# Half-array low-rank products, layer norms inside the last feed-forward, and an early read-back before the RWKV scan

## The reference

```python
a  = sigmoid(a0 + (xa @ a1) @ a2)                    # a1: 1024x64, a2: 64x1024
wl = w0 + tanh(xw @ w1) @ w2                         # twice: forward and backward, rank 64 each
g  = sigmoid(xg @ g1) @ g2                           # rank 128
kk = k * k_k, normalised per head of 64 channels
y  = scan over the tokens, forward and backward, with decay exp(-exp(.)) of each wl
```

```python
x   = layernorm(ALPHA * x + mixed @ w_out, ln1_g, ln1_b)
ffn = (silu(x @ w_gate) * (x @ w_up)) @ w_down       # hidden width 2816
x   = layernorm(ALPHA * x + ffn, ln2_g, ln2_b)       # the result
```

## Time and profile before

| | |
|---|---|
| median of three runs | 4254.95 us (4245.76 to 4255.61) |
| the profiled execution's own time | 4248.42 us |
| its span, first to last instruction | 4246.4 us, mean granted TensorE clock 0.961 |
| PE busy | 3944.9 us, 93% (weight loads 72%) |
| DVE, ACT, POOL busy | 54%, 31%, 31% |
| DMA | 361.79 MB, mean 85 GB/s |
| low-rank stage, first to last of its matmuls | 1688.0 to 1765.0 us |
| PE idle between projections and scan | 1855.8 to 1878.7 us |
| last product of the merge to first of ffn4 | 3814.5 to 3845.0 us |
| end of the last product to the end of the span | 4208.1 to 4246.4 us |

### The profile page before, as it was taken

One profiled execution on the slowest core, in us unless ns is written; L12 is line 12 of the kernel. 1 busy time (PEld: TensorE's weight loads), 2 busy tenths in 40 slices (PEclk: granted clock), 3 DMA queues, 4 the chain that ended last, 5 costly groups with the idle time before them and its releaser, 6 DMA issues. The chain is left out here.

```text
span 4246.4 us, 63005 instructions
## 1 busy us (share of the span) xinstructions
PE 3944.9 (93%) x26276; PEld 3050.7 (72%) x26276; DVE 2297.8 (54%) x3285; ACT 1310.6 (31%) x2106; POOL 1326.2 (31%) x521
## 2 busy tenths in 40 slices
PE   8999999998999998978888999899999999998997
PEld 6855788756658886456775788667777877876885
DVE  5646577466647755448885667465541526252033
ACT  3345333232213333334444333222222111103222
POOL 1011444413114440000001344345554343654442
PEclk9999999999999999889998999989999999998999
DMA  5310222222112222341112122212122121222221
GB/s 168 122 58 21 99 99 99 104 99 85 55 62 96 99 99 100 121 181 46 43 43 85 60 99 96 83 65 80 60 80 73 66 75 67 102 99 80 93 87 58
DMA packets 43517, 361.79 MB, mean 85 GB/s; under 512 B 4419, under 2 KB 4803, under 8 KB 23820
## 3 DMA queue, kind: packets, MB, share of 16 engines
q1 hardware_dynamic: 43276, 358.32, 23.3%
HBM read 334.71 MB, written 23.59 MB: 84 GB/s over the span
## 5 line engine op out<-in xcount | busy, mean ns | idle before, releaser
L266 POOL TENSOR_TENSOR ffn_weights_low<-weight_ring,ffn_weights_high 128x2048 fp32r<-128x2048 f32 x128 | 601.2, 4697 | 767.3 <-ACT ffn_weights_high L343 766.6
L192 PE MATMUL banks<-ffn_in_high,ffn_weights_low 128*128 128x512 f32 x2048 | 802.9, 392 | 31.0 <-DVE ffn_in_low L425 13.4
L193 PE MATMUL banks<-ffn_in_low,ffn_weights_high 128*128 128x512 f32 x2048 | 800.2, 391 | 0.0
L194 PE MATMUL banks<-ffn_in_high,ffn_weights_high 128*128 128x512 f32 x2048 | 799.8, 391 | 0.0
L192 PEld LDWEIGHTS banks<-ffn_in_high,ffn_weights_low 128*128 128x128 f32 x2048 | 386.4, 189 | 117.4 <-POOL ffn_weights_low L277 26.0
L193 PEld LDWEIGHTS banks<-ffn_in_low,ffn_weights_high 128*128 128x128 f32 x2048 | 386.6, 189 | 80.8 <-issue 0.7
L194 PEld LDWEIGHTS banks<-ffn_in_high,ffn_weights_high 128*128 128x128 f32 x2048 | 386.5, 189 | 80.8
L343 ACT ACTIVATE ffn_weights_high<-weight_ring 128x2048 fp32r<-128x2048 f32 x128 | 245.1, 1915 | 560.1 <-PE banks L194 560.1
L3386 POOL TENSOR_TENSOR third_weights_low<-weight_ring,third_weights_high 128x1024 fp32r<-128x1024 f32 x144 | 365.3, 2537 | 11.5
L460 DVE SCALAR_TENSOR_TENSOR ffn_gate<-ffn_up,columns_sb,ffn_gate 128x511 f32<-128x511 f32 (+1 forms) x132 | 277.6, 2103 | 161.4 <-ACT ffn_value L373 161.4
L3384 POOL CAST third_weights_high<-weight_ring 128x1024 fp32r<-128x1024 f32 x144 | 158.7, 1102 | 547.9 <-PE banks L194 499.7
(11 more groups left out here) (594 smaller groups left out, 7377.5 us busy)
## 6 DMA issues: line engine op xcount, KB each, us to landing
weight_ring<-weights SPq DMA_DIRECT2D x144, 2048.0 KB, 7.7
scan_in<-rwkv_operands SPq DMA_DIRECT2D x8, 1280.0 KB, 8.4
rwkv_operands<-rwin_staged SPq DMA_DIRECT2D x24, 256.0 KB, 3.2
scan_in<-rwkv_operands SPq DMA_DIRECT2D x8, 512.0 KB, 3.9
bias_tiles<-bias_rows SPq DMA_DIRECT2D x8, 448.0 KB, 8.8
residual<-x SPq DMA_DIRECT2D x4, 512.0 KB, 7.3
filt_decay<-decay SPq DMA_DIRECT2D x1, 2048.0 KB, 8.2
rwkv_residual<-residual SPq DMA_DIRECT2D x1, 2048.0 KB, 7.1
```

What stands on the lines that cost most here:

```text
L192: pe.matmul(out, w[1], x[0], start=start, stop=False, skip_group_check=True)
L193: pe.matmul(out, w[0], x[1], start=False, stop=False, skip_group_check=True)
L194: return pe.matmul(out, w[0], x[0], start=False, stop=stop, skip_group_check=True)
L266: pool.tensor_tensor(parts[1], landed, parts[0].bitcast(F32), ALU.subtract).then_inc(S["split"], 1)
```

## The change

**Low-rank pairs on row halves.** The two w1 matrices lie side by side in the weight chunk, a1 is laid twice, so that 24 matmuls of 128 columns replace 32; both halves of `al` and `decay` are filled. w2 of both directions stand on the two partition halves, and a2's column tiles alternate between the halves. The 24 output matmuls are issued two by two, `half(n)` being rows 0 to 63 or 64 to 127. The gather of the head sums is done twice, to partitions 0 to 15 and 64 to 79, so that the inverse norms stand on both halves; the spreads come two by two after two output matmuls. The spread matrix is loaded to both halves. ACT copies and casts whole 128-partition tiles. Bank numbers shift by one (`A2 = 3`).

**Read-back at the seam.** The scan's operand tile (`T.operands`, seven tiles) is shared with the projection, which uses it for the low-rank ring, `tanh` and `rstd`. Values are evacuated into `G.hT`. Behind its last weight load SP loads the reset row into `G.x`, then tile 0's decays and first three operands; it spills the gains of tiles 1 to 7, copies gain 0 and value 0 from SBUF to SBUF, and issues the value spills of tiles 1 to 7 with a semaphore (`T.v_spilled`) on which the block does not wait: SP waits for it in the scan before tile 1's load, DVE before it writes the first output. The scan's block starts with the mask load, without loads for tile 0.

**Layer norms inside ffn4.** `layer_norm` and `store` go; `feed_forward(..., norms=("ln1", "ln2"))` takes their work. Centring is one operation with the total in PSUM as operand. Squares are summed by 64-column matmuls that alternate between output partitions 0 to 63 and 64 to 127. DVE copies that bank, four matmuls with one column turn the sums into a 128x4 tile, on which variance, root and reciprocal work, and four matmuls with a broadcast operand and the identity spread it back; scaling reads it from PSUM. On ACT the casts of the first eight weight pieces and of the next half stand ahead of the root, two pieces ahead of the squares. Shift and cast of an input tile follow each other tile by tile.

**Down projection, in all four feed-forwards.** The last two hidden tiles are done together, bank by bank. In ffn4 DVE adds a running total behind each residual add, and one ones-matmul sums it. The output is stored in four DMAs, each after two shifted tiles.

```diff
+def norm_pe(pe, G, N, sq, gathered, inverse, bank):
+    for k in range(KT):
+        side = slice(k % 2 * (P // 2), (k % 2 + 1) * (P // 2))
+        pe.wait_ge(N["squared"], k + 1)
+        mm = pe.matmul(G.banks[side, bank, :], G.con("ones")[:, 0:P // 2], sq[:, k, :], start=(k < 2), stop=(k >= KT - 2))
+        if k >= KT - 2:
+            mm.then_inc(N["square_sums"], 1)
+    pe.wait_ge(N["gathered"], 1)
+    for j in range(JT):
+        mm = pe.matmul(G.banks[:, bank + 1, j:j + 1], gathered[:, j * P:(j + 1) * P], G.con("ones")[:, 0:1], start=True, stop=True)
+    mm.then_inc(N["columns"], 1)
+    pe.wait_ge(N["rstd_done"], 1)
+    for j in range(JT):
+        of = inverse[:, j:j + 1]
+        of = bass.AP(tensor=of.tensor, offset=of.offset, ap=[of.ap[0], [0, P]])
+        mm = pe.matmul(G.banks[:, bank + 2, j * P:(j + 1) * P], of, G.con("ident"), start=True, stop=True)
+    mm.then_inc(N["spread"], 1)
...
+def norm_centre(dve, G, N, total_bank):
+    for k in range(KT):
+        dve.scalar_tensor_tensor(out=G.x[:, k, :], in0=G.banks[:, total_bank, :], scalar=-1.0 / D, in1=G.x[:, k, :],
+                                 op0=ALU.mult, op1=ALU.add).then_inc(N["centred"], 1)
+def norm_dve(dve, G, N, gathered, inverse, bank):
+    dve.wait_ge(N["square_sums"], 2)
+    dve.tensor_copy(gathered[:, :], G.banks[:, bank, :]).then_inc(N["gathered"], 1)
+    dve.wait_ge(N["columns"], 1)
+    dve.tensor_scalar(inverse[:, :], G.banks[:, bank + 1, 0:JT], 2.0 / (P * D), LN_EPS, ALU.mult, ALU.add).then_inc(N["var_done"], 1)
+    dve.wait_ge(N["root_done"], 1)
+    dve.reciprocal(inverse[:, :], inverse[:, :]).then_inc(N["rstd_done"], 1)
+    dve.wait_ge(N["spread"], 1)
...
@@ feed_forward, SP
+            if norms:
+                for k in range(0, KT, 2):
+                    sp.wait_ge(N_out["shifted"], k + 2)
+                    sp.dma_start(G.aps["out"][k * P:(k + 2) * P, :].rearrange("(k p) n -> p k n", p=P), G.x[:, k:k + 2, :]).then_inc(S["stored"], 16)
@@ feed_forward, PE, down projection
-            for t in range(FT):
+            for t in range(FT - 2):
...
+            pe.wait_ge(S["split"], up_halves + down_halves)
+            pe.wait_ge(S["tile_split"], FT)
+            for m in (*range(4, KT), *range(4)):
+                for t in (FT - 2, FT - 1):
+                    at = t % 2 * D + m * P
+                    mm = exact_product(pe, G.banks[:, m, :], [w[:, t // 2 % 2, at:at + P] for w in w_parts],
+                                       tile_parts(t), start=False, stop=(t == FT - 1))
+                mm.then_inc(S["down_done"], 1)
@@ feed_forward, ACT
+            if norms:
+                pieces(range(2))
+                norm_squares(act, G, N_in, sq)
+                pieces(range(2, KT))
+                high(0, 0, 1, True)
+                norm_root(act, N_in, inverse)
@@ rwkv_projection, PE
-            for l, outs in enumerate(((A1,), (W0, W1), (G1,))):
+            for l in (A1, W1, G1):
...
+                for n in range(2):
+                    mm = pe.matmul(G.banks[heads(n), SUM_BANK, :], gather(m), xx_squares(m), start=(m == 0), stop=(m == KT - 1))
...
+            for n in range(A2, N_OUT, 2):
+                lora_out(n)
+                lora_out(n + 1)
                 if n >= DECAY + KT:
+                    unit_spread(n - DECAY - KT)
+                    unit_spread(n - DECAY - KT + 1)
@@ rwkv_projection, SP
+            sp.dma_start(T.operands[:, 5:7, :], of[:, 5:7, :]).then_inc(S["operands_in"], 16)
+            sp.dma_start(T.operands[:, 0:3, :], of[:, 0:3, :]).then_inc(S["operands_in"], 16)
...
+            sp.dma_start(T.operands[:, 3, :], b[:, 0, :]).then_inc(S["operands_in"], 16)
...
+            sp.dma_start(T.operands[:, 4, :], G.hT[:, 0, :]).then_inc(S["operands_in"], 16)
```

More of the change, by code:

```diff
@@ L207, in row_unit @@
     return G.chunk(c, KT)[:, 2 * u:2 * u + 2, :]
-def feed_forward(G, name, gain, taps, act_func, shift=0, keep=1.0):
+NORM = ("centred", "squared", "square_sums", "gathered", "columns", "var_done", "root_done", "rstd_done", "spread", "scaled", "shifted")
+def norm_pe(pe, G, N, sq, gathered, inverse, bank):
[15 more added lines that the diff above has]
+    mm.then_inc(N["spread"], 1)
@@ L214, in feed_forward, with norm_scale @@
+def norm_scale(dve, G, N, gain, bank, k):
+    dve.scalar_tensor_tensor(out=G.x[:, k, :], in0=G.x[:, k, :], scalar=G.col(gain, k), in1=G.banks[:, bank + 2, :],
+                             op0=ALU.mult, op1=ALU.mult).then_inc(N["scaled"], 1)
+def feed_forward(G, name, gain, taps, act_func, shift=0, keep=1.0, norms=()):
     nc = G.nc
@@ L414, in _ @@
                 high(n // 2 % 2, n // 4, n % 2, False)
+            if norms:
+                norm_squares(act, G, N_out, sq)
+                norm_root(act, N_out, inverse)
+                for k in range(KT):
+                    norm_shift(act, G, N_out, norms[1] + "_b", k)
         @block.vector
@@ L488, in _, with total @@
                 tile_low(t)
-            for n, m in enumerate((*range(4, KT), *range(4))):
+            order = (*range(4, KT), *range(4))
+            def total(n):
+                dve.wait_ge(S["added"], n + 1)
+                if n > 1:
+                    dve.wait_ge(S["totalled"], n - 1)
+                dve.tensor_tensor(square_sum, G.x[:, order[0], :] if n == 1 else square_sum, G.x[:, order[n], :], ALU.add).then_inc(S["totalled"], 1)
+            for n, m in enumerate(order):
                 dve.wait_ge(S["down_done"], n + 1)
@@ L492, in _ @@
                                          op0=ALU.mult, op1=ALU.add).then_inc(S["added"], 1)
+                if norms and n > 1:
+                    total(n - 1)
+            if norms:
+                total(KT - 1)
+                dve.wait_ge(S["total_summed"], 1)
+                norm_centre(dve, G, N_out, 4)
+                norm_dve(dve, G, N_out, rstd, inverse, 5)
+                for k in range(KT):
+                    norm_scale(dve, G, N_out, norms[1] + "_g", 5, k)
         G.first += UP_CHUNKS + DOWN_CHUNKS
@@ L2216, in _, with lora_out @@
                 pe.wait_ge(S["keys_squared"], m + 1)
-                mm = pe.matmul(G.banks[0:2 * KT, SUM_BANK, :], gather(m), xx_squares(m), start=(m == 0), stop=(m == KT - 1))
+                for n in range(2):
+                    mm = pe.matmul(G.banks[heads(n), SUM_BANK, :], gather(m), xx_squares(m), start=(m == 0), stop=(m == KT - 1))
             mm.then_inc(S["head_sum"], 1)
-            pe.wait_ge(S["select"], 32)
+            pe.wait_ge(S["select"], 48)
             arrived(pe, W2_CHUNK)
             w2 = G.ring[:, G.slot(W2_CHUNK), :]
-            for n in range(A2, N_OUT):
+            def lora_out(n):
                 if n >= LBANKS:
@@ L2448, in rwkv_scan @@
     with ExitStack() as ctx:
-        S = stage(G, "scan", ctx, "masks_loaded", "reset_loaded", "go", *PER, *PER_TURN)
-        ld = G.sb("scan_in", [P, SPILLED, SEQ], ctx=ctx)
+        S = stage(G, "scan", ctx, "masks_loaded", "go", *PER, *PER_TURN)
+        ld = T.operands
         ex = G.x[:, 0:5, :]
@@ L3285, in rwkv @@
         T.g2 = G.sb("rwkv_g2", [P, D], ctx=ctx)
-        rwkv_projection(G, T)
-        rwkv_scan(G, T)
+        T.v_spilled = ctx.enter_context(nc.semaphore("rwkv_v_spilled"))
+        with ExitStack() as inner:
+            T.operands = G.sb("scan_in", [P, SPILLED, SEQ], ctx=inner)
+            rwkv_projection(G, T)
+            rwkv_scan(G, T)
         rwkv_output(G, T)
@@ L4281, in third_block @@
             gated_merge(G, T)
-    layer_norm(G, "ln1", "ln1_g", "ln1_b", total_summed=True)
-    feed_forward(G, "ffn4", None, None, ACT.Silu, keep=ALPHA)
-    layer_norm(G, "ln2", "ln2_g", "ln2_b")
-def store(G):
-    nc = G.nc
-    with ExitStack() as ctx:
-        S = stage(G, "store", ctx, "stored")
-        block = ctx.enter_context(nc.Block())
-        @block.sync
-        def _(sp):
-            sp.dma_start(G.aps["out"].rearrange("(k p) n -> p k n", p=P), G.x[:, :, :]).then_inc(S["stored"], 16)
-            sp.wait_ge(S["stored"], 16)
+    feed_forward(G, "ffn4", None, None, ACT.Silu, keep=ALPHA, norms=("ln1", "ln2"))
 def three_blocks_kernel(nc, aps, layout):
```

228 lines of the change are left out of this document (107 added, 121 removed).

## The result

The changed kernel takes 4197.3 us (median of 4 runs, 4194.5 to 4201.8), the kernel before 4250.4 on the same chip (4 runs, 4244.9 to 4255.6): ratio 0.9871, 95% interval 0.9858 to 0.9885, 1.3% faster. A second series of the same kernel gave 0.9883 (0.9861 to 0.9905). The forecast was 4200. The profiled execution took 4198.8, span 4196.7, 49.7 us less than before.

What follows compares the result with a forecast made beforehand. PE was 93% busy, so time could come only from stretches where it stands or runs slow: 28.0 + 5.0 + 6.8 + 11.9 = 51.7 us less, forecast 4200 us, 8-in-10 range 4183 to 4222.

Steps and rivals of the forecast that it cites:

- Low-rank stage, -28.0: Low-rank stage: merged input, overlapping output pairs and a free gather bring the second projection 28.0 us earlier.
- the last four rounds [...] are about 2.2 us each on PE at 2.4 GHz: Low-rank output: four closing rounds of two row-half pairs and two tile-size switches, 2.2 us each, hidden but for 0.5.
- rival A: Low-rank output: the clock falls in the last four rounds, 17.6 us instead of 8.8; +7.3, 4207 us; chance 0.19.
- the 1.5 kept back: Low-rank stage: 1.5 us held back from the 29.5 us gain for the clock, leaving 28.0.
- Seam, -5.0: Seam to the scan: PE starts when the masks land, 1873.7 instead of 1878.7, -5.0 us.
- that wait is DMA rate: Seam to the scan: 5,888 KB in the DMA queue set the block's end, only 0.6 us less than before.
- ln1, -6.8: Layer norm into the last feed-forward: first product at 3838.3 instead of 3844.99, -6.8 us.
- So the first split waits: Last feed-forward: POOL's subtraction, running to 3837.6, holds back DVE's first split; first product 3838.3 instead of 3836.8.
- The end, -11.9: Final norm and store: first scale 4223.8 instead of 4232.1, store in four ending at 4234.5, -11.9 us.
- B: Scan seam and last feed-forward: masks land no earlier, first splits wait for two POOL operations; 4209 us; chance 0.09.
- C: Low-rank stage: pairs do not overlap in a stream; 28 us lost and 5 of the squares, 4233 us; chance 0.06.
- D: From the gather on: half-array matmuls run one by one at 1.2 GHz; +20.5, 4275 us; chance 0.04.

Runs made afterwards that it cites:

- wide spreads: Changed kernel with the eight head-norm spreads contracting over 64 rows instead of 16; time not distinguishable from the changed kernel's, the intervals overlap.
- same-half run: Changed kernel with both matmuls of each low-rank output pair contracting over rows 0 to 63; run once, 4216.7 us.

## Why the prediction was right, and where its steps were off

The way and the places of the gain were right. That the total came within 3 us of 4200 is partly luck: low-rank stage and end fell short by 4.1 and 3.0 us, seam and ln1 brought 0.8 and 2.5 more than priced, which leaves 3.8 us too little in the trace. The medians, meanwhile, lie 53.1 us apart, and four executions of the changed kernel differ by 7.3, so the agreement to a few microseconds shows nothing by itself.

**Low-rank stage, -28.0 against -23.9.** Input (-6.3 against -6.9), free gather, overlap and ACT's start 2.7 us after the gather came as worked out. The step that failed is "the last four rounds [...] are about 2.2 us each on PE at 2.4 GHz": they took 13.9 instead of 8.8, since the clock fell in the second. That is rival A's mechanism at part of its price (4.0 a round at the lower level, 4.4 in A, and not in all four); the 1.5 kept back was too little. ACT's waits for PE (1.9 and 2.8 us between the last sigmoids) are these microseconds:

```profile
1730.38 1.26 ACT L2441 ACTIVATE rwin_staged<-banks,columns_sb 128x512 f32<-128x512 f32 x2 [1.88 <-PE banks L2365]
1734.40 1.26 ACT L2441 ACTIVATE rwin_staged<-banks,columns_sb 128x512 f32<-128x512 f32 x2 [2.75 <-PE banks L2365]
```

A pair was priced at 0.97 and costs 0.86, and 27.16 us for 32 matmuls are 0.849 each, not 0.858; neither matters for the sum. The prediction weighed the Trainium skill's rule that the clock follows how busy PE has been (TensorE: Matmul & The Clock Gate, "What's actually happening") against the earlier trace rows; the wide spreads kept 1.00 at 80% busy, so here too the traces do not follow busyness alone.

**Seam, -5.0 against -5.8.** The sequence was right, and the block's end too, to 0.1 us after the last product. But "that wait is DMA rate" is only in part its cause: 2 MB less in the queue brought 4.3 us of 5.2, and with the direct tiles and the value spills gone as well it was 1.1 more, with a spill's landing last. The masks landed 5.6 us after the block's end, at about 1844.7, level with the keys. The prediction has them 6.7 us after it, and its own terms (4.5, 2.0 and 0.7) make 7.2.

**ln1, -6.8 against -9.3.** "So the first split waits" did not occur. POOL's pieces were priced at 1.06, from a stretch where DVE worked beside them; here they take 0.69, 3 us less in eight. The bound "-9.5 if the split passes" was the case. The rule of the Trainium skill (SBUF — State Buffer, "Who interferes with whom"), an exclusive lock for the whole instruction, holds twice when POOL is late (3.68 and 4.95 us for 0.69 of work). But it did not speak against casting ahead, as I had it: casting ahead is what takes POOL out of DVE's way.

**The end, -11.9 against -8.9.** The first scale came 7.7 us earlier (8.3 predicted) and the last store landed 3.0 us after its issue, 1.2 sooner than 4.2. The step that failed is the tail: "the last 512 KB take 3.9 to 4.2" (4.55 in the sum) counts to the landing as if it were the end, and leaves out the stage's retirement, 51 clears at 0.071 us. I counted what the store issues on SP, and not the semaphores of the stage that it moved into.

**Rivals.** B is out (masks moved forward, splits passed). C is out by the same-half run: taking the 64-row overlap away costs 5 us. C's own price of 28 us is not tested by it, since the gather and the 16-row pairs still overlapped there. D is out: half-array matmuls overlapped on both levels of the clock (a pair every 0.86 us, and 2.0 at the lower level with its switch).

## What to carry to other kernels

When work moves into another stage, its semaphores move too: look in the records, behind the last landing and behind each change of stage, for what the busy views don't count; here clearing by ranges was worth about 12 us by the distances in the traces, for a few lines. Price an operation by a row with the same neighbours running. And when a stage is made faster, ask first which transfer its length had been hiding.

## What was not expected of the hardware

- Semaphore clears on POOL follow each other every 0.071 us; one for a range took 0.31 us at 265 us into the span, where 50 single ones had taken 3.8.
- A PE wait of 2.4 us for POOL's clears was followed by products at the lower clock (0.79 over 8 us), one of 0.6 us was not (1.00).
- Two 64-row fp32 matmuls of 512 columns on opposite row halves took 0.86 us together at 2.4 GHz, 0.87 each one by one.
- Wide spreads in place of 16-row ones: granted clock 1.00 instead of 0.55 in the rounds.
- A spill of 768 KB needed 14.2 us to land with 5.9 MB issued in all, 10.6 with 3.8 MB, and 10.7 with 3.3 MB; 256 KB from SBUF to SBUF 11.2. In a filled queue a small transfer is not a fast one.
- The same code differs between profiles by up to 10 us within the first 255 us of the span, and by up to 14 from the scan to the merge; what happens in it stays open.
